# Modulation products in plain fp32 from unsplit weights, K tiles in four column groups, partial rows added by the next product

## What is computed

```
silu_c, silu_cc = silu(c), silu(c_ctx)            # two vectors of 2048
mod  = silu_c  @ w_mod[l] + b_mod[l]              # 2048 x 6144 weights: shift, scale, gate
cmod = silu_cc @ w_mod[l] + b_mod[l]
h  = rmsnorm(x,  norm_g[l]) * (1 + scale)  + shift
hc = rmsnorm(cx, norm_g[l]) * (1 + cscale) + cshift
... u = h @ w_in, uc = hc @ w_in, mixers, y ...
x = x + gate * (y @ w_o[l]);   cx = cx + cgate * (yc @ w_o[l])   # cx in layer 0 only
```

## Time and profile before

| what | value |
|---|---|
| median of 3 runs | 2709.29 us (2704.67 to 2714.11) |
| the profiled execution, its own time | 2709.09 us |
| its span | 2707.3 us |
| granted TensorE clock, mean share of full | 0.981 |
| PE, DVE, ACT busy | 95%, 52%, 48% of the span |

### The profile page before, as it was taken

One profiled execution on the slowest core, in us unless ns is written; L12 is line 12 of the kernel. 1 busy time (PEld: TensorE's weight loads), 2 busy tenths in 40 slices (PEclk: granted clock), 3 DMA queues, 4 the chain that ended last, 5 costly groups with the idle time before them and its releaser, 6 DMA issues. The chain is left out here.

```text
span 2707.3 us, 32472 instructions
## 1 busy us (share of the span) xinstructions
PE 2572.9 (95%) x12228; PEld 2009.2 (74%) x12228; DVE 1412.3 (52%) x2245; ACT 1298.0 (48%) x1967; POOL 221.1 (8%) x314
## 2 busy tenths in 40 slices
PE   6999999999999999999999999999988999999888
PEld 2566777777778766677777677977877887888776
DVE  6644444455553555475565545566554544444454
ACT  6644333334443444464454444545555445654543
POOL 1000001001000000000112100101110001101100
PEclk9999999999999999999999999999998999999999
DMA  9667534333222665557545444755554566567543
GB/s 323 241 219 233 184 101 124 102 97 110 86 82 86 227 221 186 175 182 240 158 154 176 128 140 163 229 165 189 173 181 134 186 208 214 175 191 232 166 155 133
DMA packets 230091, 464.80 MB, mean 172 GB/s; under 512 B 17346, under 2 KB 42240, under 8 KB 228656
## 3 DMA queue, kind: packets, MB, share of 16 engines
q1 hardware_dynamic: 208560, 390.73, 44.8%
q0 software_dynamic: 20832, 67.81, 7.9%
q10 hardware_dynamic: 544, 4.19, 0.4%
HBM read 431.89 MB, written 30.77 MB: 171 GB/s over the span
## 5 line engine op out<-in xcount | busy, mean ns | idle before, releaser
L1321 DVE TENSOR_TENSOR w_lo<-raw,w_hi 128x1024 fp32r<-128x1024 f32 (+4 forms) x762 | 898.5, 1194 | 1018.8 <-ACT w_hi L1046 1017.1
L1851 PE MATMUL pp<-w_hi,hT_hi 128*128 128x512 f32 (+3 forms) x2904 | 1176.1, 405 | 2.9 <-DVE w_lo L1321 2.2
L1853 PE MATMUL pp<-w_hi,hT_lo 128*128 128x512 f32 (+3 forms) x2904 | 1120.5, 386 | 0.0
L1852 PE MATMUL pp<-w_lo,hT_hi 128*128 128x512 f32 (+3 forms) x2904 | 1119.3, 385 | 0.0
L1046 ACT ACTIVATE w_hi<-raw 128x1024 fp32r<-128x1024 f32 (+4 forms) x762 | 772.6, 1030 | 702.3 <-PE pp L1853 673.8
L1851 PEld LDWEIGHTS pp<-w_hi,hT_hi 128*128 128x128 f32 x2904 | 551.1, 190 | 144.3 <-issue 42.2
L1853 PEld LDWEIGHTS pp<-w_hi,hT_lo 128*128 128x128 f32 x2904 | 549.6, 189 | 107.0
L1852 PEld LDWEIGHTS pp<-w_lo,hT_hi 128*128 128x128 f32 x2904 | 551.8, 190 | 96.3 <-issue 7.2
L1846 PE MATMUL pY<-w_hi,cT 128*4 128x512 f32 x384 | 158.6, 413 | 24.9 <-DVE w_lo L1321 12.3
L1847 PE MATMUL pY<-w_lo,cT 128*4 128x512 f32 x384 | 157.9, 411 | 0.0
L1202 ACT ACTIVATE arena<-pY 128x512 f32<-128x512 f32 (+2 forms) x114 | 62.1, 545 | 139.9 <-PE pY L2005 108.5
(11 more groups left out here) (269 smaller groups left out, 1739.2 us busy)
## 6 DMA issues: line engine op xcount, KB each, us to landing
raw<-in_w_mod_dram SPq DMA_DIRECT2D x192, 512.0 KB, 4.9
raw<-in_w_in_dram SPq DMA_DIRECT2D x168, 512.0 KB, 3.6
raw<-in_e_w_in_dram SPq DMA_DIRECT2D x104, 512.0 KB, 3.6
raw<-in_w_o_dram SPq DMA_DIRECT2D x64, 512.0 KB, 3.7
raw<-in_o_w_in_dram SPq DMA_DIRECT2D x64, 512.0 KB, 3.8
raw<-in_w_out_dram SPq DMA_DIRECT2D x64, 512.0 KB, 3.6
raw<-in_w_in_dram SPq DMA_DIRECT2D x56, 440.0 KB, 3.5
scratch_u<-ust POOLq DMA_DIRECT2D x35, 512.0 KB, 3.8
```

The source lines that it names most:

```text
L1321: dve.tensor_tensor(w_lo[:, g.n % SPLIT, 0:n], raw[:, g.n % RAW, 0:n], w_hi[:, g.n % SPLIT, 0:n].bitcast(F32), ALU.subtract).then_inc(lo_d ...
L1851: pe.matmul(dst, hT_hi[:, kk, o:o + P], hi[:, k, :], start=a, stop=False)
L1852: pe.matmul(dst, hT_hi[:, kk, o:o + P], lo[:, k, :], start=False, stop=False)
L1853: ins = pe.matmul(dst, hT_lo[:, kk, o:o + P], hi[:, k, :], start=False, stop=z)
```

## The change

1. Modulation groups are no longer split. PE multiplies `raw` itself by `cT`, now plain fp32 with 2 columns, one product per K tile. K tile K goes to column group K mod 4: its two result rows land in pY at partition 32 * (K mod 4), so a chunk leaves four pairs of partial rows, each the sum of four K tiles.
2. Splitting counts only the other groups (`W.cut`, number `g.s`, issued at `split_at`). SP waits, for a modulation slot of `raw`, until PE has finished the group (`quanta`).
3. ACT copies four pairs of rows from pY to `parts` (zeroed once, so that the rest of its 128 rows adds nothing), four instructions instead of one. The bias is row 2 of `parts`, one buffer: its load waits for the `cols` of the chunk before.
4. `cols` uses rows 0 to 97 of `parts`; the selector adds the four partial rows and the bias. It now exists for gate chunks too, there as one product of 98 rows by 2 columns with 512 moving columns into pO, which ACT copies to `rows`; `gate` reads those 2 rows instead of 5. The DVE instruction that made the low half of `cT` goes.

```diff
 Work: +        self.cut = [g for g in self.groups if g.ch.kind != "mod"]
+            g.split_at = max(self.cut[n - SPLIT].q1 if n >= SPLIT else 0, self.groups[max(0, g.n - AHEAD)].q0)
 schedule:
-                if ch.block is not None:
-                    add(ch.q1 + 1, "cols", ch.name)
+                add(ch.q1 + 1, "cols", ch.name)
 SP:
-                    sp.wait_ge(lo_done, g.n - RAW + 1)
+                    p = groups[g.n - RAW]
+                    if p.ch.kind == "mod":
+                        sp.wait_ge(quanta, p.q1)
+                    else:
+                        sp.wait_ge(lo_done, p.s + 1)
 POOL, bias:
+                if n >= 1:
+                    pool.wait_ge(filled["O"], left["O", ("cols", mods[n - 1])])
+                pool.dma_start(parts[2:3, :], D["b_mod"][...]).then_inc(bias_here, 16)
 ACT, evac of a modulation chunk:
-                    act.activation(rows[r:r + 4, s, :], src[0:4, :], ACT.Copy).then_inc(done, 1)
+                    for r in (0, 32, 64, 96):
+                        ins = act.activation(parts[r:r + 2, :], src[r:r + 2, :], ACT.Copy)
+                    ins.then_inc(done, 1)
 ACT, new cols (gate chunks only):
+                act.wait_ge(filled["O"], left["O", ("cols", name)])
+                r = 32 * ch.row
+                act.activation(rows[r:r + 2, :], pO[0:2, :], ACT.Copy).then_inc(freed["O"], 1)
 PE, new:
+            def mod_quantum(g):
+                ch, slot = g.ch, g.n % RAW
+                pe.wait_ge(raw_here[slot], 16 * (g.n // RAW + 1))
+                if g.j == 0:
+                    begin("Y", "acc", ch.name, 0)
+                for k, K in enumerate(g.ks):
+                    r = 32 * (K % 4)
+                    ins = pe.matmul(pY[r:r + 2, :], cT[:, K, :], raw[:, slot, 512 * k:512 * k + 512], start=K < 4, stop=K >= 12)
+                ins.then_inc(quanta, 1)
 PE, cols:
+                p = parts[0:98, :]
+                if C[name].block is None:
+                    pe.matmul(b[0:2, :], keep[0:98, C_SEL:C_SEL + 2], p, start=True, stop=True).then_inc(filled["O"], 1)
+                    return
                 for k in range(4):
-                    ins = pe.matmul(b[:, 2 * k:2 * k + 2], rows[r:r + 5, s, 128 * k:128 * k + 128], keep[r:r + 5, C_SEL:C_SEL + 2], start=True, stop=True)
+                    ins = pe.matmul(b[:, 2 * k:2 * k + 2], p[:, 128 * k:128 * k + 128], keep[0:98, C_SEL:C_SEL + 2], start=True, stop=True)
 PE, gate:
-                    pe.matmul(b, keep[r:r + 5, c:c + 128], rows[r:r + 5, s, :], start=True, stop=True)...
+                    pe.matmul(b, keep[r:r + 2, c:c + 128], rows[r:r + 2, :], start=True, stop=True)...
```

More of the change, by code:

```diff
@@ L859, in setup @@
                 pool.memset(half_neg, -0.5).then_inc(setup_done, 1)
-                pool.wait_ge(setup_done, 1)
+                pool.memset(parts[:, :], 0.0).then_inc(setup_done, 1)
+                pool.wait_ge(setup_done, 2)
             def bias(name):
[L864 to L874, removed]
+                ch, n = C[name], mod_n[name]
+                if n >= 1:
+                    pool.wait_ge(filled["O"], left["O", ("cols", mods[n - 1])])
+                pool.dma_start(parts[2:3, :], D["b_mod"][ch.layer:ch.layer + 1, ch.c0:ch.c0 + 512]).then_inc(bias_here, 16)
             def store(name, half):
@@ L1111, in evac, with cols @@
                     act.activation(pair, pair, ACT.Silu).then_inc(silued, 1)
+            def cols(name):
+                ch = C[name]
+                if ch.block is not None:
+                    return
+                act.wait_ge(filled["O"], left["O", ("cols", name)])
+                if ch.layer == 1:
+                    act.wait_ge(filled["X0"], left["X0", ("gate", f"out0_{ch.row}")])
+                    act.wait_ge(filled["X1"], left["X1", ("gate", f"out0_{ch.row}")])
+                r = 32 * ch.row
+                act.activation(rows[r:r + 2, :], pO[0:2, :], ACT.Copy).then_inc(freed["O"], 1)
             def sq_x(t):
@@ L1304, in _ @@
             setup()
-            for g in groups[:AHEAD]:
-                split(g)
+            ahead = 0
             for q, todo in enumerate(plan.at):
@@ L1310, in _ @@
                         mine[e[0]](*e[1:])
-                if q < NQ and slots[q][1] == 0 and slots[q][0].n + AHEAD < len(groups):
-                    split(groups[slots[q][0].n + AHEAD])
+                while ahead < len(W.cut) and W.cut[ahead].split_at <= q:
+                    split(W.cut[ahead])
+                    ahead += 1
         @block.vector
@@ L1771, in _ @@
                     "g_log": g_log, "g_less": g_less_, "g_finish": g_finish, "fl_add": fl_add, "fl_min": fl_min_}
-            setup()
-            for g in groups[:AHEAD]:
-                split(g)
+            ahead = 0
             for q, todo in enumerate(plan.at):
@@ L1874, in gate @@
                     c = C_SEL + 2 + 128 * v
[L1875 removed]
+                    pe.matmul(b, keep[r:r + 2, c:c + 128], rows[r:r + 2, :], start=True, stop=True).then_inc(filled[f"X{v}"], 1)
             def x_turn(l, K, t0):
```

89 lines of the change are left out of this document (39 added, 50 removed).

## The result

| | before | after |
|---|---|---|
| median | 2707.99 us (2704.67 to 2716.63, 6 runs) | 2730.14 us (2725.04 to 2734.27, 6 runs) |
| span of the profiled execution | 2707.3 us | 2732.5 us |
| granted clock, mean | 0.981 | 0.969 |

The ratio is 1.0073, with a 95% interval of 1.0053 to 1.0093: the changed kernel is 0.7% slower. The forecast was 2667 us and faster.

What follows compares the result with a forecast made beforehand. PE was taken to bound the kernel, busy for 2572.9 of 2707.3 us. The terms -51 + 18 + 7 - 2 - 14 = -42 us, from 2709.09 us, gave 2667 us; the range was 2644 to 2712.

Steps and rivals of the forecast that it cites:

- Part 1: Modulation products behind the opening: four column groups run at once, 0.90 us per pair of groups, minus 51 us.
- 64-row visit: Earlier-trace row for products in two row groups: switching costs about 0.3 us per visit, a bound of plus 20 us.
- A: Rival for the modulation products: column groups don't overlap at all, time 2876 us; chance 0.11.
- B: Rival for the modulation products: only neighbours overlap, K tiles follow at 0.43 us, time 2741 us; chance 0.08.
- Part 2: Chunk ends behind the opening: PE waits about 1.1 us for ACT's four copies, plus 18 us (9 to 34).
- part 3: Small items: the gate chunks' new `cols` plus 7 us (bounds 6 and 10), layer 1's `cols` minus 2.
- Part 4: The opening: without the split, PE's lag and ACT's blocking go, minus 14 us (bounds 0 and minus 22).
- Part 5: Queues: later freeing of `raw` slots and the single bias buffer cost nothing; 28 or 5 us if they did.
- Rival C: Overlap as forecast but paid back: switches +20, ACT late at chunk ends +16, no opening gain +14 us.
- near end: Rival C coming out near zero, the case counted as the same time; chance 0.07.
- The 0.19 for "slower": Chance that the changed kernel is slower, with A at 0.11 and B at 0.08.
- far end: Rival C with all 50 us paid back: -42 + 50 = +8 us.

Runs made afterwards that it cites:

- warm_ends: The changed kernel plus five products of no use at each opening chunk's end, under the four copies: 2724.26 us, ratio 1.0053 to the kernel before.
- one_copy: The changed kernel with ACT copying rows 0 to 97 in one instruction instead of four, bias in row 98: 2690.09 us, ratio 0.9926 to the kernel before.
- late_cols: The changed kernel with the adding product two slots later in the mixed stretches, one in the opening: 2697.01 us, ratio 0.9953 to the kernel before.
- late_one: The changed kernel with both late_cols and one_copy: 2678.58 us, ratio 0.9875 to the kernel before.
- hybrid: late_one with the opening's eight modulation chunks split and computed as in the kernel before: 2682.05 us, ratio 0.9882 to the kernel before.
- late_one_ring8: late_one with 8 landing slots for weights instead of 6, and 3 buffers of split weights instead of 4: 2681.34 us, ratio 0.9888 to the kernel before.
- warm: The changed kernel plus products of no use in the opening, after quanta 3 to 6 and at each modulation chunk's end: 2745.14 us, ratio 1.0129.

## Why the prediction was wrong

The forecast was -42 us; the traces differ by +25 and the medians by +22. By its own steps:

**Part 1, the products** (forecast -51). The mechanism held: four records at once, 0.43 us per round. The term failed by its size, and at the place where I chose between two rows. I took a visit to have no edges, as the present products of 4 columns have none, over the 0.3 us of the 64-row visit. The edges are there, 0.32 per visit (0.09 entering, 0.10 before the return, 0.13 behind it), within 0.02 of the earlier trace rows. A pair gained 0.68, not 0.96. The full stretches show -36.6 in the quanta themselves and 8.9 back in others: some -27. Of the 24 us that are missing, 68 visits at 0.32 are 22. The Trainium skill, "TensorEngine Tiling (Array Packing)", Key Properties, says that changing the tiling mode drains the engine; I had put the sum by that rule some 20 us smaller, and it came out about 24 smaller. The nearer row was not the one with the same shape of product, but the one that also ran several tiles at once.

**Rivals A and B** fell, as the earlier trace rows had said. The Trainium skill, "TensorE: Matmul & The Clock Gate", Part 3, The mechanism, has matmuls keep their order at start and end. Whole products do keep that order here as far as the records tell. But all second halves start after the fourth tile's first half (the starts at 214.17 and 214.60), so for the halves of fp32 products in different column groups, as rival B took the rule, the trace does not agree. (B's terms add to 2743 us, not 2741.)

**Part 2, the evacuation, with the gate's product of part 3** (forecast +18 +7 -2 = 23). Measured +33. I took 0.48 between two copies, the distance to the next instruction on ACT in the earlier trace rows; the copies followed at 0.60. The wait I put at 1.1 was 1.00 at a clean end, and that near hit is partly luck. The terms of my sum (0.56 + 0.2 + 2.0) give 2.8 and not 2.9 us until pY is free; the slower copies add 0.36 to it, and the edges of the visit, which I had put at nothing, lengthen PE's cover by about as much. The failed term is the end where ACT has splits ahead: gate1_3 alone costs 6.7 us (2.34 of waiting, and a lower clock behind it) where I had 2.0. The eight gate ends cost 24 us together against 16, the eight of layer 1 9 against 7. A busy ACT (34) and the switch around the gate's product (10) were named as bounds, and the milder values taken.

**Part 4, the opening** (forecast -14, bounds -22 to 0). Measured +20 (22.1 less the 2.5 of the earlier start). This step failed in sign, and it is the largest miss of the four. It took for granted that without the split ACT would no longer be held before the copy. ACT was held still, by b_q0's splits, and the copies came at 73.02, 4.1 us after the products' end; PE's idle time for the evacuation (copies and adding product) grew from 10.5 to 16.5 us, and landing took the place of the split (16.9 and 8.8 against 12.7). It also gave chunk ends 3 us for the first spell in all and no more for the others. But in the opening nothing covers the copies: the next chunk starts at once in the same bank, or, at a spell's end, b_q0 runs one quantum and the adding product then waits. I charged the lower clock with 4 us for three b_q0 spells; the changed kernel took 5.1, 4.1 and 6.9 us longer over them (21.43, 19.99 and 33.65 us against 16.31, 15.85 and 26.72), waits included. warm_ends shows 14 us to hang on the clock, one_copy with late_cols 25 on the copies and their place. These overlap: the copies make PE stand, and standing brings the clock down. late_one and hybrid show the other half of the error. The 9 us that I saw in the first spell are there (8, at b_q0), but the 8 of the other two spells are not, and at b_q1 nothing is left of either (-5.7 against -5.4).

**Part 5, queues** (0). Bias loads landed in 6.7 us at worst and cost nothing, as forecast. The ring's smaller reach cost about 4 us in the opening and about as much in scale1_0, by the trace of late_one_ring8; so in the full stretches the zero did not quite hold. The times of the whole do not tell either from nothing.

**Rival C** had the right shape, overlap as forecast but paid back, with 0.07 for its near end. I gave it 20 + 16 + 14 = 50 to pay back; it was 24 + 10 + 34 = 68, to which the opening brought half because its bound stopped at zero gain. A bound on a step that adds waits to a stretch where PE already waits has to reach into loss. The 0.19 for "slower" stood on A and B alone, which both fell; a kernel slower because its overlap is paid back had no chance in it, although C's far end stood at +8.

From b_q1 to d_kv late_one gains 26 us, and my terms for the full stretches added to -28. That is no confirmation: the -28 has 18 us of waits for copies in it, which late_one does not have. Without them the forecast would be -46, and the difference is again about the size of the edges.

## What to carry to other kernels

When work is spread over column groups, plan the collection first. Partial rows in four places want one copy over all partitions, not one each, and the product that adds them must stand far enough behind that copy in the order; these two edits turned 0.7% slower into 1.2% faster, and part of that is the order, which helps the kernel before as well. Join visits to another tiling where buffers allow, as each pays its edges once (0.33 us per join in the trace; over the whole kernel the gain was not shown). In a stretch where the array already waits for data, a longer serial tail can do more than its own length: here the projection behind it ran at the lower clock. Work of no use in front of real work made this kernel slower (warm); under waits that were there anyway it bought the clock back in the trace (warm_ends), and the time by less than the runs can tell.

## What the runs showed of the hardware that was not expected

- A copy by ACT of 2 rows of 512 from the accumulation bank takes 0.59 us, of 98 rows 0.60 us, and four of them take 2.39.
- In four column groups the first halves of four fp32 products start within 0.02 us and their second halves 0.43 later. From a pair's start to the projection's return it is 0.97 us, and 3.53 with all four products in one column group.
- Entering and leaving the column groups costs 0.32 us per visit, whether it holds two quanta or four; a pair of groups with the 4-column fp32r products at column 0 costs 0.03, in the quantum behind it.
- PE held at a clock of 1.00 from 60 to 80 and 100 to 120 us (warm), against 0.67 and 0.59, did not by itself make the kernel faster.
